# Sample attention of a hybrid decoder layer, unrolled so that one pair's scores stand beside the last pair's values

## The reference

```python
def cmp_branch(q, kc, vc, q_pos):
    ...
    sc = jnp.einsum('btkgd,bnkd->btkgn', q, kc) * ATTN_SCALE
    p = softmax_masked(sc, avail[None, :, None, None, :])
    ...
    return o, jnp.sum(p, axis=3)
...
    return lax.top_k(pri, min(TOP_N, n_sel))[1]
...
def sel_branch(q, kg, vg, idx, q_pos):
    ...
    p = softmax_masked(sc.reshape(b, t, h, NSA_GROUP, kk * sb), mask)
...
def win_branch(q, kw, vw, q_pos, k_pos):
    diff = q_pos[:, None] - k_pos[None, :]
    mask = (diff >= 0) & (diff < WINDOW) & (k_pos[None, :] >= 0)
```

## Time and profile before

| | us |
|---|---|
| median of 3 runs | 1334.09 (1333.64 to 1341.03) |
| the profiled execution | 1331.47 |
| its span | 1329.7 |
| sample attention, first turned keys to the prompt's first matmul | 469.37 to 619.88 |
| PE busy in the span | 1170.7 (88%) |
| DVE, ACT, POOL busy | 638.0, 395.4, 123.2 |

### The profile page before, as it was taken

The page is one execution under the profiler, slowest core; times in us unless marked ns, Lnnn a source line. Parts: engine busy times, 40 slices in busy tenths (PEclk is TensorE's granted clock), DMA queues, the critical chain, the costliest instruction groups (busy, mean ns, idle before and its releaser), DMA issues.

```text
span 1329.7 us, 19913 instructions
## 1 busy us (share of the span) xinstructions
PE 1170.7 (88%) x7709; PEld 1028.5 (77%) x7709; DVE 638.0 (48%) x1384; ACT 395.4 (30%) x809; POOL 123.2 (9%) x216
## 2 busy tenths in 40 slices
PE   4899998899888688987778859799999999989996
PEld 2799998888655444555466649799999999989995
DVE  3336434442344644434565561466566656672221
ACT  3224322232111133221354540232332333252222
POOL 3000200010000000000222240000000000000000
PEclk9999999998687788888787769999999999989998
DMA  8521335343012144403100013203222322233221
GB/s 205 168 64 33 116 113 206 133 135 127 5 52 95 45 190 162 161 3 114 28 0 0 0 63 126 66 24 108 66 65 73 122 65 66 61 89 83 60 75 71
DMA packets 88720, 114.40 MB, mean 86 GB/s; under 512 B 19231, under 2 KB 79749, under 8 KB 86300
## 3 DMA queue, kind: packets, MB, share of 16 engines
q1 hardware_dynamic: 82587, 70.85, 17.4%
q0 software_dynamic: 6080, 42.83, 8.6%
HBM read 103.32 MB, written 13.85 MB: 88 GB/s over the span
## 4 chain that ended last, share of the span: by engine, by line
PE 82%; DVE 11%; ACT 3%; issue 2%; DMA 1%; SPq 0%; ACTq 0%; DVEq 0%; POOL 0%; POOLq 0%; PEldq 0%
PE banks L1326 12%; PE banks L1324 10%; PE banks L969 6%; PE banks L1361 6%; PE banks L916 5%; PE banks L1360 4%; PE banks L919 3%; PE banks L920 3%; PE banks L1149 3%; PE banks L1252 3%; PE banks L1232 3%; PE banks L1297 2%; PE banks L953 2%; PE banks L1201 2%; PE banks L1296 2%
## 5 line engine op out<-in xcount | busy, mean ns | idle before, releaser
L1324 PE MATMUL banks<-xnT_r,RB_r 128*128 128x256 f32 x352 | 103.8, 295 | 9.1 <-DVE RC_r L537 9.1
L1326 PE MATMUL banks<-RC_r,RB_r 128*128 128x320 f32 x352 | 110.1, 313 | 0.0
L1326 PE MATMUL banks<-xnT_r,RB_r 128*128 128x320 f32 x352 | 110.0, 313 | 0.0
L1326 PE MATMUL banks<-xnT_r,ring_r 128*128 128x320 f32 x352 | 109.9, 312 | 0.0
L1324 PE MATMUL banks<-xnT_r,ring_r 128*128 128x256 f32 x352 | 99.2, 282 | 0.0
L1324 PE MATMUL banks<-RC_r,RB_r 128*128 128x256 f32 x352 | 99.2, 282 | 0.0
L969 PE MATMUL banks<-RA,RB 128*128 128x128 f32 (+1 forms) x576 | 83.9, 292 | 5.9 <-DVE RA L1579 3.8
L969 PEld LDWEIGHTS banks<-RA,RB 128*128 128x128 f32 x576 | 76.4, 203 | 9.9 <-DVE RA L1579 5.4
L1324 PEld LDWEIGHTS banks<-xnT_r,RB_r 128*128 128x128 f32 x352 | 67.5, 192 | 11.6 <-issue 7.7
L1324 PEld LDWEIGHTS banks<-xnT_r,ring_r 128*128 128x128 f32 x352 | 67.8, 193 | 0.0
L1324 PEld LDWEIGHTS banks<-RC_r,RB_r 128*128 128x128 f32 x352 | 67.7, 192 | 0.0
(11 more groups left out here) (561 smaller groups left out, 2986.9 us busy)
## 6 DMA issues: line engine op xcount, KB each, us to landing
ring<-in_w_up_dram SPq DMA_DIRECT2D x22, 1024.0 KB
ring<-in_w_down_dram SPq DMA_DIRECT2D x8, 1408.0 KB, 6.9
ring<-in_w_in_dram SPq DMA_DIRECT2D x9, 1024.0 KB, 5.3
RB<-in_state_win_dram SPq DMA_DIRECT2D x8, 512.0 KB, 12.5
ring<-in_w_out_dram SPq DMA_DIRECT2D x2, 2048.0 KB
out_win_s_dram<-in_state_win_dram POOLq DMA_DIRECT2D x1, 4032.0 KB
xsp<-RC SPq DMA_DIRECT2D x1, 2304.0 KB, 13.0
xT<-xsp SPq DMA_DIRECT2D x1, 2304.0 KB, 9.1
```

The lines of the kernel that those rows point to most:

```text
L1324: t.matmul(ps[4 + par][:, w * UA:(w + 1) * UA], wk[:, w, k, c], x[:, k, 0:UA], skip_group_check=True, **first)
L1326: last = t.matmul(ps[2 * w + par][:, 0:UB], wk[:, w, k, c], x[:, k, UA:T], **on)
```

## The change

The stage is written out as five rounds, with no loop. Round `p` scores pair `p` while it turns the weights of pair `p - 1` and multiplies them with the values. The two batches stand side by side: a block `q` of 512 rows is turned for both (`turn_keys`), copied by ACT into one of four slots of `KTb`, and scored by two matmuls, the first batch into partitions 0 to 63 of a bank, the second into 64 to 127. The products with the values are two matmuls of 64 weight columns against 128 value columns where one of 128 against 256 stood. There are five row slots, the third of them `xT`, which is loaded back only after the stage. ACT copies two of the four groups of turned weights, DVE the others. The five copies of operands are gone, and the result is scaled in three instructions; it is stored by four DMAs. The reading back of results is issued ahead of `w_out`.

```diff
-        slots = [ring[:, 0, :], ring[:, 1, :], ring2[:, 0, :], ring2[:, 1, :]]
+        slots = [ring[:, 0, :], ring[:, 1, :], xT[:, :, :].rearrange("p k t -> p (k t)")[:, 0:ROWF], ring2[:, 0, :], ring2[:, 1, :]]
+        SLOT_OF = [0, 1, 2, 3, 4, 0, 1, 2]
...
-            for b in range(2, NB):
-                if b >= 4:
-                    pool.wait_ge(S("s_pv"), b // 2 - 1)
-                g.indirect_dma_start(slots[b % 4], None, pool_sel,
-                                     bass.IndirectOffsetOnAxis(ap=idx[:, b:b + 1], axis=0)).then_inc(S(f"sel_in{b % 4}"), 16)
+            selected_rows(3)
+            selected_rows(4)
+            pool.wait_ge(S("s_pv"), 1)
+            selected_rows(5)
+            selected_rows(6)
+            pool.wait_ge(S("s_pv"), 2)
+            selected_rows(7)
...
+            exp_cmp(0)
+            for p in range(5):
+                if p < 4:
+                    keys(p, 0)
+                if p:
+                    exp_sel(p - 1, 1)
+                    weights_act(p - 1, 1)
+                if p < 4:
+                    keys(p, 1)
+                if p < 3:
+                    exp_cmp(p + 1)
+                if p < 4:
+                    keys(p, 2)
+                if p:
+                    exp_win(p - 1)
+                    weights_act(p - 1, 3)
+                if p < 4:
+                    keys(p, 3)
+                    keys(p, 4)
+                    exp_sel(p, 0)
...
-                    for n in range(10):
-                        if 1 <= n < 9:
-                            turn_keys(n + 1)
-                        score(n)
...
-                    for j in range(16):
-                        if j % 4 == 0:
-                            pe.wait_ge(S("s_pt"), p4 + (j // 4 + 1))
-                        t.matmul(ps[0][:, 0:256], PT[:, j, :], both[:, :, j, 1, :], start=(j == 0), stop=False)
-                    t.matmul(ps[0][:, 0:256], PTn[:, 0, :], vnp[:, :, 0, :], start=False, stop=True).then_inc(S("s_pv"), 1)
...
+            def turn_keys(p, q):
+
+                for b2 in range(2):
+                    n, b = 10 * p + 2 * q + b2, 2 * p + b2
+                    if n >= 2:
+                        pe.wait_ge(S("s_kt"), n - 1)
+                    if q == 0:
+                        pe.wait_ge(S(f"sel_in{SLOT_OF[b]}"), sel_count[b])
+                    if q == 4 and b2 == 0:
+                        pe.wait_ge(S(f"win_in{p % 2}"), 32 * (p // 2 + 1))
+                    src, j0 = (slots[SLOT_OF[b]], 4 * q) if q < 4 else (wkv[:, 2 * (p % 2) + b2, :], 0)
+                    for j in range(4):
+                        last = t.transpose(ps[2 + n % 2][:, j * P:(j + 1) * P],
+                                           src[:, (j0 + j) * 256:(j0 + j) * 256 + P], ident[:])
+                    last.then_inc(S("s_t"), 1)
+
+            def score(p, q):
+
+                m = 5 * p + q
+                pe.wait_ge(S("s_kt"), 2 * m + 2)
+                if m >= 2:
+                    pe.wait_ge(S("s_ev"), m - 1)
+                for b2 in range(2):
+                    last = t.matmul(ps[m % 2][batch_rows(b2), :], Qbd[:, 2 * p + b2, :], KTb[:, (2 * m + b2) % 4, :],
+                                    start=True, stop=True)
+                last.then_inc(S("s_sc"), 1)
...
+            def values_sel(p, j0, j1):
+
+                if p and j0 == 0:
+                    pe.wait_ge(S("s_out"), p)
+                for j in range(j0, j1):
+                    if j % 8 == 0:
+                        pe.wait_ge(S("s_ptd"), 3 * p + j // 8 + 1)
+                    if j % 8 == 4:
+                        pe.wait_ge(S("s_pta"), 2 * p + j // 8 + 1)
+                    for b2 in range(2):
+                        t.matmul(ps[6][batch_rows(b2), 0:P], PT[:, j, batch_rows(b2)],
+                                 slots[SLOT_OF[2 * p + b2]][:, 256 * j + P:256 * j + 2 * P], start=(j == 0), stop=False)
...
+            score_few(0)
+            for p in range(5):
+                if p < 4:
+                    turn_keys(p, 0)
+                if p:
+                    turn_sel(p - 1, 0)
+                    turn_sel(p - 1, 1)
+                if p < 4:
+                    score(p, 0)
+                    turn_keys(p, 1)
+                    if p == 0:
+                        few_turned(0)
+                    if p < 3:
+                        score_few(p + 1)
+                    score(p, 1)
+                    turn_keys(p, 2)
+                if p:
+                    turn_sel(p - 1, 2)
+                    turn_sel(p - 1, 3)
+                if p < 4:
+                    score(p, 2)
+                    turn_keys(p, 3)
+                if p:
+                    turn_win(p - 1)
+                few_turned(p + 1)
+                if p:
+                    values_sel(p - 1, 0, 4)
+                if p < 4:
+                    score(p, 3)
+                    turn_keys(p, 4)
+                if p:
+                    values_sel(p - 1, 4, 16)
+                    values_rest(p - 1)
+                if p < 4:
+                    score(p, 4)
...
+            cmp_max(0)
+            cmp_scaled(0)
+            pick_blocks(0)
+            for p in range(5):
+                if p:
+                    weights_dve(p - 1, 0)
+                if p < 4:
+                    masked(p, 0)
+                if p < 3:
+                    cmp_max(p + 1)
+                if p < 4:
+                    masked(p, 1)
+                if p:
+                    weights_dve(p - 1, 2)
+                if p < 3:
+                    cmp_scaled(p + 1)
+                if p < 4:
+                    masked(p, 2)
+                if p:
+                    weights_win(p - 1)
+                if p < 3:
+                    pick_blocks(p + 1)
+                if p < 4:
+                    masked(p, 3)
+                if p:
+                    rows_out(p - 1)
+                if p < 4:
+                    masked_win(p)
...
-            sp.dma_start(xT[:, :, :].rearrange("p k t -> p (k t)"), xsp).then_inc(S("rows_moved"), 16)
...
-                sp.wait_ge(S("s_out"), p + 2)
-                sp.dma_start(osc[:, p * P:(p + 1) * P, :].rearrange("w r d -> r w d"), orow).then_inc(S("s_sto"), 16)
                 if p < 2:
+                    sp.wait_ge(S("s_pv"), p + 1)
                     window(p + 2)
+                sp.wait_ge(S("s_out"), p + 1)
+                for q in range(4):
+                    r, c0 = 32 * q, HD * (q % 2)
+                    sp.dma_start(osc[:, p * P + r:p * P + r + 32, :].rearrange("w r d -> r w d"),
+                                 orow[r:r + 32, :, c0:c0 + HD]).then_inc(S("s_sto"), 16)
+            sp.wait_ge(S("s_sto"), 16 * 16)
...
+            sp.dma_start(xT[:, :, :].rearrange("p k t -> p (k t)"), xsp).then_inc(S("rows_moved"), 16)
```

More of the change, by code:

```diff
@@ new lines, in keys, with exp_cmp @@
+            def keys(p, q):
+                for n in range(10 * p + 2 * q, 10 * p + 2 * q + 2):
+                    act.wait_ge(S("s_t"), n + 1)
+                    if 5 * p + q >= 2:
+                        act.wait_ge(S("s_sc"), 5 * p + q - 1)
+                    a.activation(KTb[:, n % 4, :], ps[2 + n % 2], ACT.Copy).then_inc(S("s_kt"), 1)
+            def exp_cmp(p):
+                act.wait_ge(S("s_cb"), p + 1)
+                for b2 in range(2):
+                    r = slice(64 * b2, 64 * b2 + 64)
+                    last = a.activation(pcd[r, r], ps[7][r, 16:80], ACT.Exp, bias=cols[p % 2][r, 0:1], scale=SCALE,
+                                        accum_out=cols[p % 2][r, 1:2])
+                last.then_inc(S("s_ce"), 1)
@@ new lines, in exp_sel, with exp_win @@
+            def exp_sel(p, half):
+                if half == 0:
+                    act.wait_ge(S("s_sb"), p + 1)
+                c0, c1 = ((0, 1024), (1024, PAST + TS))[half]
+                a.activation(Ss[:, c0:c1], Ss[:, c0:c1], ACT.Exp, bias=cols[p % 2][:, 3:4], scale=SCALE,
+                             accum_out=cols[p % 2][:, 6 + half:7 + half]).then_inc(S("s_se"), 1)
+            def exp_win(p):
+                act.wait_ge(S("s_wb"), p + 1)
+                a.activation(Sw, Sw, ACT.Exp, bias=cols[p % 2][:, 2:3], scale=SCALE,
+                             accum_out=cols[p % 2][:, 5:6]).then_inc(S("s_we"), 1)
@@ L1204, in _, with batch_rows @@
-            pe.wait_ge(S("s_out"), 5)
+            def batch_rows(b2):
+                return slice(64 * b2, 64 * b2 + 64)
+            def turn_keys(p, q):
[12 more added lines that the diff above has]
+                    last.then_inc(S("s_t"), 1)
@@ new lines, in few_turned @@
+            def few_turned(p):
+                if p < 4:
+                    pe.wait_ge(S("s_pn"), p + 1)
+                if p > 2:
+                    pe.wait_ge(S("s_ptd"), 3 * (p - 2))
+                if p > 1:
+                    last = t.transpose(ps[7][0:TS, 256:384], Ss[:, PAST:PAST + TS], ident[:])
+                    last = t.transpose(ps[7][0:TS, 384:512], Sw[:, WIN:WIN + TS], ident[:])
```

(15 more changed lines are left out.)

316 lines of the change are left out of this document (125 added, 191 removed).

## The result

The changed kernel took 1287.68 us in the median of four runs (1278.28 to 1300.22), the one before 1333.87 beside it: a ratio of 0.963 (95% interval 0.951 to 0.975), or 1285.1 us against the 1334.09 shown. The ratios of this document leave out, as slow, runs over 1.5% above the fastest of their kernel, here the 1300.22. The four runs are 1278.28, 1278.52, 1296.84 and 1300.22: two groups, and the median lies where no run does. By the two medians, with all four runs, it would be 0.965 or 1287.9 us, just inside the range.

What follows compares the result with a forecast made beforehand. PE, the chain for 82% of the span, was held by the order of work; rounds and epilogue summed to 115.2 us against 150.5, so 1331.47 - 35.3 = 1296.2, plus 2.6 for the median: forecast 1299 us, range 1287 to 1320.

Steps and rivals of the forecast that it cites:

- Halves overlap fully: Scores and values: matmuls of 64 weight columns into different halves of the partitions overlap fully; five score pairs take 5.5 us.
- the rival was priced at: Scores and values: halves do not overlap at full clock, costing 36 us, all of the gain; 1335 us, chance 0.09.
- The order rival: Scores: the second half starts only in order, a score pair takes 1.28 us, 7 us more; 1306 us, chance 0.10.
- Rounds of 20 us: Sample stage: round 0 20.1 us, round 1 20.5; rounds 2 and 3 31.4 each with 8.5 stall and 2.4 clock.
- The 5.4 us at the lower clock behind a restart: PE after a pause: runs at 1.2 GHz for 5.4 us, costing 2.4 us in each of rounds 2 and 3.
- Gathers share the transfer: Rival: batches 5, 6 and windows land together, round 2 stalls 4.5 us longer, round 3 1.5; 1305 us, chance 0.13.
- The clock stays low in the mix: Rival: the mix of work leaves PE at 1.2 GHz in rounds 1 to 3; 1360 us, chance 0.04.
- Epilogue: End of the stage: last weights, turnings, values and scaling after the rounds take 11.8 us.
- The stage's sum: Sample stage: 20.1 + 20.5 + 31.4 + 31.4 + 11.8 = 115.2 us against 150.5, 35.3 us less.
- `w_out` and `xT` hidden: Moved DMAs behind the stage: `w_out` lands at +25 us, wanted at +30.4; the `xT` reload costs nothing within 180 us.
- the last one: Whole kernel: profiled execution 1331.47 less the stage's 35.3 gives 1296.2 us; the median is 2.6 above it.
- The range: Whole kernel: low 1287 us from shorter gathers, value passes and round 0; high 1320 from order, shared gathers, late `w_out`, thin cover.

Runs made afterwards that it cites:

- experiment 4: Changed kernel with the 16 value products of one batch first, then the other's 16, instead of alternating; ratio 0.976, stage 130.2 us.
- Experiment 3: Changed kernel without the gathers of batches 5 and 7, which read other batches' slots (part of the result wrong); median 1272.85 us, ratio 0.960.
- experiment 6: Changed kernel with PE's two waits inside each mLSTM head filled with extra products; 1281.15 us, ratio 0.973, stage 116.0 us.
- experiment 12: Kernel before the change with only the reload of `xT` moved behind the loads of the output weights; 1335.82 us, ratio 1.000.
- experiment 1: Changed kernel timed again with no edit, beside the kernel before; median 1296.97 us, ratio 0.979.
- experiment 2: Changed kernel with the gather of batch 2 issued behind the mixing of the mLSTM heads, not in the compression; ratio 0.970.

## Why the prediction was right, and where it failed

- **Halves overlap fully: right.** The two passes of a pair start within 0.01 us of each other (516.86), a score pair takes 1.01 us, and with both batches on one half the stage grows by 33.0 us of the 36 that the rival was priced at. The order rival does not hold: a score pair would take 1.28 by it, and in experiment 4 a second batch's pass starts ahead of three earlier ones. The Trainium skill, "TensorE: Matmul & The Clock Gate", Part 3, The mechanism, has matmuls start in strict program order; the trace of experiment 4 does not agree.
- **Rounds of 20 us: right** in sum, 21.5 for round 0 and 19.7 for round 1, together 0.6 over the forecast. In rounds 2 and 3 PE waits 8.55 and 8.73 for the slots, forecast 8.5 each. A round took 30.4, not 31.4. Experiment 3 took the wait away and 22.1 us from the two rounds, forecast 21.8: 17.3 of waiting and 4.8 of lower clock, 2.4 a round, as the sum had it. What was 1 us too long is the round itself, 19.5 and 19.2 where 20.5 stood. (The 5.4 us at the lower clock behind a restart was a misreading of the earlier trace rows, where a mean of 0.68 over 3 us makes it 6.1; here it was 4.7, from 504.31 to 509.0: the clock is 0.50 from 504.5 to 507.5 and 0.75 in the next 3 us.)
- **Gathers share the transfer: no.** Round 2 waited 0.2 us less than round 3, where the rival had 3 us more.
- **The clock stays low in the mix: no.** PEclk is 1.00 in round 1 and 0.83 in rounds 2 and 3, where the waits are.
- **Epilogue: 1.5 us too short** (13.3), with PEclk 0.87; at full clock it is the 11.7 of experiments 3 and 6, forecast 11.8. What failed in it is the clock, which the sum left at full.
- **The stage's sum, 115.3 against 115.2, is partly luck.** Its five terms are off by +1.4, -0.8, -1.0, -1.0 and +1.5, which cancel, and with another clock the same stage takes 4.5 us less (experiment 6).
- **`w_out` and `xT` hidden: right**; no instruction of ScalarE up to 720 us waits for a DMA, and experiment 12 shows the second within its interval of 0.6%.
- **The failed step is the last one**: "Against the profiled execution: 1331.47 - 35.3 = 1296.2". It takes the rest of the program as fixed, and above all the clock of the mLSTM heads. One profiled execution was the base, its heads in the low-clock pattern. Of the four runs of the changed kernel in the comparison two had, by their times, the other one (two of three in the ratio), and of the four of the kernel before (1325.35 to 1341.03) none. With 15 us less in the heads, the stage as forecast and 2.5 less behind it, the profiled run of the changed kernel took 1278.28 where 1296.2 stood. Kernels of either sort show both patterns in their profiles: the changed one first and in experiment 1, the kernel before in its own profile and in experiment 12. The kernel before ran from 1315.12 to 1340.09 in the 23 runs beside experiment 12. With like heads, 1278.4 stands to 1315.3 (0.972) and 1297 to 1333 (0.973); forecast was 0.974. The ratio measured first, 0.963, and that of experiment 1, 0.979, lie on both sides of it. The range had no term for this spread: its low end was built from the stage alone, and 15 us of clock in untouched code were more than all its terms. That the draw took the time out of the range and not back into it is chance.
- **What stays open**: what decides the heads' pattern in a run, why some runs lie between the groups (1291.20 in experiment 2, 1322 to 1328 in the kernel before), and what holds the half-clock stretch in each filled head.

What the sum did not ask is what each part was worth. By one profile each, and so to some 4 us, the halves give 33; unrolling, slots and the rest up to 7.5 (155.4 less 33.0 less 114.9); the pipeline takes 5.6 back, since it puts the release of a slot at a round's end and its use at the next one's start. The 7.5 is a remainder and was not measured by itself. The forecast had the stall, but not that an order without it would be as good or better, nor that the same pipeline with its values earlier gives 16.3 over that order.

## What to carry to other kernels

Before a forecast, take the spread of runs as a term of its own: look for stretches at half clock in code that the change leaves alone, and price them both ways; profile more than one execution, and let the median of a few runs in two groups count for little. When a software pipeline moves the last use of a buffer to the end of a round and the first use of its refill to the start of the next, count the refill against that gap, and move the last use forward; here this was worth 22 us of a stage of 120. Give two half-width matmuls different halves of the array and alternate them one by one; in blocks only the seam overlaps.

## What the runs showed of the hardware

Matmuls with 64 weight columns into different halves of the partitions overlap at full clock nearly without loss (0.109 us a pair of 128-column passes, where one alone took 0.107; 1.01 us for two f32 scores of 512, as for one), and a pass of the later one started three passes ahead of its turn (experiment 4). Seventeen waits of up to 0.74 us for ScalarE in four rounds left the clock at 1.00; one of 8.55 us was followed by 0.50. A wait that was filled with products did not always keep the clock: with 20 products ahead of the stage the low stretch began at 445 in place of 441 us, and the stage was 6.6 us longer. Code that no edit touched took 95.7 or 106.7 us, with the clock, from one execution to the next.
